# C and D attention of an encoder step: own keys in two column stretches, later keys prepared inside the loop, bias loaded behind the first keys and queries

## The reference, cut to what matters

```python
def attend(q, k, v, bias, mask, sink=None):          # C: windowed, 8 query heads, 2 key heads
    s = jnp.einsum('bqhgd,bkhd->bhgqk', qg, k).astype(F32) * (d ** -0.5)
    s = s.reshape(b, hq, tq, -1) + bias
    s = jnp.where(mask, s, NEG_INF)
    ...                                              # softmax over the keys and the sink, then p @ v
...
def dsa_attend(q, qi, wi, qpos, k, v, ki, kpos, topk, t5_d):   # D: one shared key head
    _, sel = lax.top_k(score, topk)                  # 256 keys per query, chosen by an indexer
    ...                                              # scores of the chosen keys + bias, softmax, times v
```

## Time and profile before

| what | value |
|---|---|
| median of 3 runs | 3963.08 us (3957.71 to 3964.36) |
| the profiled execution: time / span | 3964.57 us / 3962.8 us |
| busy over the span: PE, DVE, ACT, POOL | 92%, 52%, 41%, 18% |
| mean granted TensorE clock | 0.965 |
| C stage, first transfer issued to last output | 2891.1 to 3089.5 us |
| C stage, ahead of the first `scores` | 2891.1 to 2932.1 us |
| D stage, first transfer issued to first `scores` | 3092.6 to 3135.1 us |
| D loop | 3135.1 to about 3705 us |

### The profile page before, as it was taken

The page is one execution under the profiler, slowest core; times in us unless marked ns, Lnnn a source line. Parts: engine busy times, 40 slices in busy tenths (PEclk is TensorE's granted clock), DMA queues, the critical chain, the costliest instruction groups (busy, mean ns, idle before and its releaser), DMA issues. The chain is left out here.

```text
span 3962.8 us, 51485 instructions
## 1 busy us (share of the span) xinstructions
PE 3645.3 (92%) x18001; PEld 2626.6 (66%) x18001; DVE 2065.5 (52%) x5049; ACT 1630.9 (41%) x2532; POOL 693.9 (18%) x474
## 2 busy tenths in 40 slices
PE   5999999996999999998899988899959699999798
PEld 3899989995777666665786654444436465556576
DVE  4211111117887445433331469999958577777522
ACT  5101100013545444443331459998447344444432
POOL 5100000002223111110341100000022332222342
PEclk9999999997999999999999999999979799999899
DMA  6212211214344322321542111101242411100343
GB/s 220 63 68 68 67 66 68 68 57 108 88 109 106 73 68 57 72 51 31 196 162 84 58 39 58 55 33 66 86 113 77 102 36 26 27 24 19 142 164 117
DMA packets 197665, 315.75 MB, mean 80 GB/s; under 512 B 18960, under 2 KB 140200, under 8 KB 191712
## 3 DMA queue, kind: packets, MB, share of 16 engines
q1 hardware_dynamic: 151152, 227.06, 19.5%
q10 hardware_dynamic: 38448, 61.88, 4.3%
q0 software_dynamic: 7824, 23.72, 2.6%
HBM read 207.24 MB, written 105.35 MB: 79 GB/s over the span
## 5 line engine op out<-in xcount | busy, mean ns | idle before, releaser
L1043 PE MATMUL attAB_p_o<-attAB_pt,attAB_v 128*65 128x512 f32 (+4 forms) x1120 | 431.1, 482 | 0.2 <-ACT attAB_pt L1091 0.2
L1131 DVE TENSOR_REDUCE attAB_mx<-attAB_p_s 128x1 f32<-128x512 f32 (+2 forms) x360 | 209.6, 609 | 297.7 <-PE attAB_p_s L976 187.2
L517 DVE COPY ab_stage<-ab_pA 128x256 f32<-128x256 f32 (+2 forms) x108 | 52.7, 488 | 586.6 <-PE ab_pA L486 544.8
L2568 DVE TENSOR_SCALAR_CACHE_REDUCE cd_junk<-score,cd_thr 128x512 bf16<-128x512 f32 (+8 forms) x288 | 350.4, 1275 | 1.4 <-DVE cd_thr L2585 0.3
L2606 ACT ACTIVATE cd_side<-score,cd_thr 128x384 bf16<-128x384 f32 (+2 forms) x192 | 322.3, 1679 | 23.8 <-DVE cd_thr L2585 16.5
L515 ACT ACTIVATE ab_stage<-ab_pA 128x256 f32<-128x256 f32 (+2 forms) x108 | 47.1, 436 | 674.1 <-PE ab_pA L486 655.6
L484 PE MATMUL ab_pA<-ab_W_hi,h_hi 128*128 128x256 f32 x1088 | 309.1, 284 | 3.4 <-PE ab_pA L486 3.2
L1019 PE MATMUL attAB_p_t<-attAB_q_a,attAB_k_a 128*128 128x512 f32 (+4 forms) x560 | 300.3, 540 | 12.7 <-DVE attAB_s_t L1178 11.3
L485 PE MATMUL ab_pA<-ab_W_lo,h_hi 128*128 128x256 f32 x1088 | 307.9, 283 | 0.0
L486 PE MATMUL ab_pA<-ab_W_hi,h_lo 128*128 128x256 f32 x1088 | 307.8, 283 | 0.0
L1672 PE MATMUL attD_p_o<-attD_pt,attD_v 128*65 128x512 f32 (+1 forms) x548 | 282.0, 595 | 1.2 <-ACT attD_pt L1761 1.1
(11 more groups left out here) (353 smaller groups left out, 8538.1 us busy)
## 6 DMA issues: line engine op xcount, KB each, us to landing
ab_W_raw<-in_w_ab SPq DMA_DIRECT2D x17, 1024.0 KB, 5.8
attAB_raw<-t_k SPq DMA_DIRECT2D x32, 544.0 KB, 6.4
attAB_raw<-t_q SPq DMA_DIRECT2D x32, 544.0 KB, 8.4
mix_o<-t_o SPq DMA_DIRECT2D x34, 512.0 KB, 4.3
mix_gate<-t_gate SPq DMA_DIRECT2D x68, 256.0 KB, 4.7
norm_x<-in_x ACTq DMA_DIRECT2D x17, 512.0 KB, 4.3
t_gate<-ab_stage ACTq DMA_DIRECT2D x68, 128.0 KB, 1.7
t_v<-ab_stage ACTq DMA_DIRECT2D x68, 128.0 KB, 1.7
```

The lines of the kernel that those rows point to most:

```text
L1043: done = nc.tensor.matmul(p_o[u % 2][0:VW, i0 * w:(i0 + n) * w], left, pt[c % NPT][:, at * w:(at + n) * w], start=(c == plan.chunks_of[u][ ...
L2568: nc.vector.tensor_scalar(junk[nth % 2][:, 0:widths[n]], sc[n][:], T[:, n:n + 1], None, ALU.is_ge, ALU.add, accum_out=cnt[s % 2][:, n:n + ...
```

## The change

The own keys of 2176 columns are cut at column 768 (six tiles of 128). The key items are ordered: first stretch of every group, second stretch of every group, cached keys of every group. Each item has a semaphore and a place of its own, so no load waits for a split; POOL no longer splits query block 0, DVE does (`split_first_queries`); in C the cached keys have raw tiles of their own, in D the second raw tile.

```diff
+        KEY_CUT = 6 * P
+        own_cols = (slice(0, KEY_CUT), slice(KEY_CUT, ROWS))
+        items = [(g, 0) for g in kvs] + [(g, 1) for g in kvs] + [(g, "cached") for g in kvs]
+        late_at = dict(zip({"C": (4, 6, 10, 12), "D": (3, 24)}[kind], range(NK, 3 * NK)))
+        FIRST_FILLS = 1 if kind == "C" else 2
+
+        def item_needed(u):
+            g, b = group(u % 2), plan.block[u // 2]
+            if b == LAST:
+                return items.index((g, "cached"))
+            return items.index((g, 0 if (b + 1) * P <= KEY_CUT else 1))
...
-                    nc.gpsimd.tensor_tensor(q_a[s][HD:P], q_raw[b % NRAW][HD:P], q_a[s][HD:P].bitcast(F32), ALU.subtract
-                                            ).then_inc(q_split, 1)
+                    if b:
+                        pool.wait_ge(q_split, b)
+                        nc.gpsimd.tensor_tensor(q_a[s][HD:P], q_raw[b % NRAW][HD:P], q_a[s][HD:P].bitcast(F32), ALU.subtract
+                                                ).then_inc(q_split, 1)
...
-                        if u < NK:
-                            pe.wait_ge(key_split, 2 * u + 1)
-                        if plan.block[b] == LAST and x == 0:
-                            pe.wait_ge(key_split, len(items))
+                        pe.wait_ge(key_split, item_needed(u) + 1)
...
+                pe.wait_ge(ident_in, N_IDENT)
-                turn_bias()
...
                     for f in plan.fills_of[u]:
                         fill(f)
+                        if f + 1 == FIRST_FILLS:
+                            turn_bias()
...
                 round_keys(0)
-                for b in plan.early_blocks:
-                    round_queries(b)
-                for m in range(1, len(items)):
+                round_queries(0)
+                for m in range(1, NK):
                     round_keys(m)
...
                 for c in range(NT):
                     exponent(c)
+                    if c in late_at:
+                        round_keys(late_at[c])
...
-                keep_bias()
-                split_keys(0)
-                for m in range(1, len(items)):
-                    split_keys(m)
+                split_keys(0)
+                split_first_queries()
+                for m in range(1, NK):
+                    split_keys(m)
                 for u in plan.early:
                     for f in plan.fills_of[u]:
                         reduce(f)
+                        if f + 1 == FIRST_FILLS:
+                            keep_bias()
                     negate(u)
...
+                    if c in late_at:
+                        split_keys(late_at[c])
```

More of the change, by code:

```diff
@@ L1362, in attention_by_blocks @@
         raw = [sb(f"raw{k}", [P, ROWS]) for k in pair]
+        cached_raw = [sb(f"cached_raw{g}", [P, n_cache * P]) for g in kvs] if kind == "C" else raw[1:2]
         k_a = [sb(f"k_a{g}", [P, ROWS], F32R) for g in kvs]
@@ L1405, in attention_by_blocks @@
             "sink_less", "sink_out", "sinks_set"))
-        raw_in = [sem(f"raw_in{k}") for k in pair]
+        key_in = [sem(f"key_in{m}") for m in range(3 * NK)]
+        ident_in = sem("ident_in")
         q_in = [sem(f"q_in{k}") for k in range(NRAW)]
@@ L1409, in attention_by_blocks, with item_tiles @@
         o_stored = [sem(f"o_stored{k}") for k in pair]
-        N_CONST = 48
+        N_CONST = 32 if kind == "C" else 16
+        N_IDENT = 16 if kind == "C" else 32
         FIXED = 4 * NK + 2 + 2
-        items = [(g, n) for g in kvs for n in range(2)]
+        KEY_CUT = 6 * P
[8 more added lines that the diff above has]
+            return items.index((g, 0 if (b + 1) * P <= KEY_CUT else 1))
+        def item_tiles(m):
+            g, n = items[m]
+            if n == "cached":
+                return cached_raw[g], slice(0, n_cache * P), (c_a[g], c_b[g])
+            return raw[g], own_cols[n], (k_a[g], k_b[g])
         chunks_of_block = lambda b: range(plan.chunks_of[2 * b][0], plan.chunks_of[2 * b + 1][-1] + 1)
@@ L1418, in key_loads @@
             g, n = items[m]
-            if m >= 2:
-                sp.wait_ge(key_split, m - 1)
-            own, cached = key_srcs(g)[0:2]
+            tile, cols, _ = item_tiles(m)
+            src = key_srcs(g)[1] if n == "cached" else key_srcs(g)[0][:, cols]
             for half in (slice(0, HD), slice(HD, P)):
-                if n == 1:
-                    sp.dma_start(raw[m % 2][half, 0:n_cache * P], cached).then_inc(raw_in[m % 2], 16)
-                else:
-                    sp.dma_start(raw[m % 2][half, :], own).then_inc(raw_in[m % 2], 16)
+                sp.dma_start(tile[half, cols], src).then_inc(key_in[m], 16)
         def query_loads(sp, b):
@@ L1476, in _ @@
                     sp.dma_start(sink[:], d.sinks.broadcast_to([P, HEADS])).then_inc(consts, 16)
-                else:
-                    sp.dma_start(identb[:], d.identb).then_inc(consts, 16)
-                key_loads(sp, 0)
-                query_loads(sp, 0)
+                for m in range(1, NK):
+                    key_loads(sp, m)
+                query_loads(sp, 1)
+                for m in range(NK, 2 * NK):
+                    key_loads(sp, m)
                 if kind == "D":
-                    for b in range(NMASK):
+                    for b in range(1, NMASK):
                         mask_loads(sp, b)
-                query_loads(sp, 1)
-                for m in range(1, len(items)):
-                    key_loads(sp, m)
                 for b in range(2, NRAW - 1):
                     query_loads(sp, b)
+                for m in range(2 * NK, 3 * NK):
+                    key_loads(sp, m)
                 for b in range(2, NB):
@@ L1552, in _ @@
                     prepare(b)
+                if kind == "D":
+                    pool.wait_ge(bias_kept, 4)
                 for b in plan.early_blocks:
@@ L1717, in round_keys @@
                 def round_keys(m):
-                    g, n = items[m]
-                    act.wait_ge(raw_in[m % 2], 32 * (m // 2 + 1))
-                    hi, w = ((k_a, ROWS), (c_a, n_cache * P))[n]
-                    nc.scalar.activation(hi[g][:], raw[m % 2][:, 0:w], ACT.Copy).then_inc(key_rounded, 1)
+                    tile, cols, (hi, _) = item_tiles(m)
+                    act.wait_ge(key_in[m], 32)
+                    nc.scalar.activation(hi[:, cols], tile[:, cols], ACT.Copy).then_inc(key_rounded, 1)
                 def round_queries(b):
@@ L1778, in _ @@
                         keep_mask(b, k)
+                for b in plan.early_blocks[1:]:
+                    round_queries(b)
                 for u in plan.early:
@@ L1901, in _ @@
                 dve.wait_ge(fixed, FIXED)
-                dve.wait_ge(consts, N_CONST)
+                dve.wait_ge(ident_in, N_IDENT)
                 nc.vector.tensor_copy(ident_r[:], ident[:]).then_inc(ident_kept, 1)
+                split_keys(0)
+                split_first_queries()
+                for m in range(1, NK):
+                    split_keys(m)
                 if kind == "C":
+                    dve.wait_ge(consts, N_CONST)
                     for k in pair:
```

19 lines of the change are left out of this document (13 added, 6 removed).

## The result

| | before | after |
|---|---|---|
| median | 3961.40 us (4 runs, 3957.71 to 3964.36) | 3936.13 us (4 runs, 3934.65 to 3938.47) |
| ratio after to before | | 0.9936, 95% interval 0.9923 to 0.9948 |
| the profiled execution: span | 3962.8 us | 3933.7 us |
| mean granted TensorE clock | 0.965 | 0.968 |

The forecast started from 3963.08, the median of three executions before; with the fourth it is 3961.40. From 3963.08, the 25.3 us would have led to 3937.8, just inside the range: that the time falls outside is partly chance, the 6.9 us by which the gain was underestimated are not. One execution of the experiment e10 took 7679 us at a granted clock of 0.48 and is left out of its median.

The account below looks back on a forecast made before the run. PE is saturated in the C and D loops but mostly waits ahead of them, so work removed there is worth its time. Gains 8.9 + 14, less loop costs 3 and 1.5, give 18.4 us: 3963.08 to 3945, range 3937 to 3957.

Parts of the forecast that it names:

- C start, -8.9: Ahead of the C loop: unit 2 filled at 2917.3 instead of 2926.17, 8.9 us earlier; bounds 7.5 and 11.5.
- 11.5 us if it lands at 2911: Upper bound of C's start gain: query block 1 lands once only its bytes and the value loads are through.
- D start, -14: Ahead of the D loop: first `scores` at 3121.1 against 3135.07, 14 us earlier; bounds 11.5 and 17.
- I take 3107: Ahead of the D loop: assumed landing time of the bias, between 3104.3 as lower bound and 3109.
- equal shares: D's bias transfer: queues served in turn, values taking half while both are queued; bias at about 3109, sum 2 us smaller.
- PE's first fills behind the turning hold it about 1 us: Ahead of the D loop, after the bias lands: PE's fills delay the first `scores` by about 1 us.
- C loop, +3: Rounding and splitting late keys inside the C loop makes PE lose 3 us; bounds 0 and 7.1.
- D loop, +1.5: Late key work at steps 3 and 24 of the D loop costs 1.5 us; bounds 0.5 and 7.2.
- A, loops in full: Rival, both loops: PE waits for every rounding and split, 14.3 us, giving 3954.5; chance 13%.
- B, late transfers: Rival: D's bias lands at 3109 and C's query block 3 at 2932, 5 us late, giving 3951.7; chance 14%.
- C, slower by the clock: Rival: four large late splits each stop PE until its clock falls, 13.6 us more, giving 3968; chance 3%.
- D, no effect: Rival: something unseen holds each stage's first `scores`, within 4 us of before, giving 3961; chance 5%.

Follow-up runs that it names:

- e10: Changed kernel with SP issuing the value loads behind query blocks 1 to 3, and all four far fills of D's unit 0 ahead of the bias turning; 3933.2 us, 0.9921.
- e2: C stage as changed, D stage written by the former function; 3952.4 us, ratio 0.9978 to the kernel before.
- e3: D stage as changed, C stage written by the former function; 3949.3 us, ratio 0.9963 to the kernel before.
- e4: Changed kernel's order of loads, but all key items rounded and split ahead of the loops, none inside; 3971.6 us, ratio 1.0023 to the kernel before.
- e7: Changed kernel with the value loads issued by SP behind query blocks 1 to 3, instead of by POOL beside the bias; 3933.2 us, 0.9922.
- e1: The changed kernel run again without edit; 3938.1 us, ratio 0.9943 to the kernel before.
- e11: The changed kernel run once more without edit, on another occasion; 3937.3 us, ratio 0.9930 to the kernel before.
- e6: Changed kernel with each late key item rounded twice on ACT and split twice on DVE; 3965.8 us, ratio 1.0005 to the kernel before.
- e9: Changed kernel with late key items rounded and split twice, D's cached keys at step 20 instead of 24; 3960.2 us, ratio 0.9995.

## Why the prediction was right and wrong

**Right: what bounds.** Work ahead of the loops was worth its time and work inside them nearly nothing. e2 and e3 show the gain of each stage by itself, e4 that the new order of loads brings none of it without the move into the loop.

**C start, -8.9, measured -9.5 (-8.3 to -10.7 in the other executions).** The steps hold: block 1 was forecast at 2913.7, T0 + 22.6, and came at T0 + 20.4 to 22.8. e7 shows that its bound, "11.5 us if it lands at 2911, when its bytes and the value loads alone are through", left out the larger lever: with the value loads out of the way, the start is 16 us shorter than before.

**D start, -14, measured -17.3 (-18.4 to -18.7 in e1, e3 and e11). This step failed by size.** Its mechanism was right, two of its terms were not. First, "I take 3107", the landing of the bias at T0 + 14.4: measured T0 + 12.1, near the lower bound that I worked out and passed over (the bytes alone, 3104.3, T0 + 11.7). I had let the value loads of POOL's queue go ahead of the bias. The DMA rows by queue (packets, MB, share), q1 for SP and q0 for POOL, from T0 to the bias, show how far they did. Of the changed kernel:

```profile
q1 hardware_dynamic: 3008, 2.40, 69.0%
q0 software_dynamic: 50, 0.20, 9.8%
```

and of e6, the one execution of this order where the bias came at T0 + 16.0, with all issues ahead of it within 0.4 us of the same times:

```profile
q1 hardware_dynamic: 3193, 2.50, 56.8%
q0 software_dynamic: 261, 0.91, 27.9%
```

0.20 MB of values against 0.91, while SP's queue moved about the same. The others lie between: 0.21 (e1), 0.20 (e11), 0.34 (e3) and 0.49 MB (e9). So the landing lies on either side of what I took: T0 + 12.0 to 12.5 in five of the six executions in which the turning waits for this load alone (the changed kernel, e1, e3, e9 and e11), 16.0 in one. What makes the difference is open. The Trainium skill, "DMA: Bandwidth & Descriptors", section Queues, rings and completion order, has the engines serve queues with work in turn, packet by packet. By equal shares the prediction had made the landing 2 us later than its value. The executions with 0.20 MB do not show equal shares; e6, with 27.9% of the time against 56.8%, comes nearer to them.

Second, "PE's first fills behind the turning hold it about 1 us": no hold, DVE never waited over 0.16 us behind the first copy (8.46 us where 8.7 and 1 were forecast). Together 2.3 + 1.2 = 3.5 us, against the 3.3 that were missing; it is measured from the first reduce, 0.16 us behind the last bias copy. In e1, e3 and e11, where PE reached full clock earlier, the stretch from the bias to `scores` is another 1.0 to 1.2 us shorter.

**C loop, +3, measured +0.8 (0.1 to 1.3 against e4, with e2).** Oversized by 2.2 us: the second term that was mis-sized. I had added up delays of PE of 0.9, 1.4 and 2.0 us over steps 5 to 9. The rows show 0.56 us at step 5 and 0.66 two steps behind the second split: at step 4 DVE was idle for 1.99 us ahead of its split, waiting for ACT, and still caught up; it has 21.4 us of idle time in the 133.

**D loop, +1.5, measured +0.7 (0.2 to 1.1 against e4, 2.9 in e3).** Of the right size in the changed kernel's executions. The 2.9 of e3 come from what the walk left out: DVE's split at step 3 was stretched by POOL's.

**The sum.** 3.3 us of D's start, 2.2 of C's loop, 0.8 of D's loop and 0.6 of C's start are 6.9, which is what the medians miss (25.3 and 18.4). All four errors have one sign: each time I had taken a value on the dear side. Luck worked against the forecast in one more place: the median before fell by 1.7 us with its fourth execution. The range's lower end, 3937, was 2 us above the bounds that I had worked out myself (3935).

**The rivals.** A, loops in full: refuted, the loops grew by 0.8 and 0.7 us where it has 14.3. B, late transfers: block 3 was in time in the changed kernel, ACT rounds it without a wait. But the late bias that B assumed, T0 + 16.4, is what e6 had (16.0): this half of B is real, and came in one of six executions. C, slower by the clock: the mechanism is real. In e9 half clock followed waits of 1.46 and 3.20 us, the latter close to the 2.91 of the earlier trace rows, and in e6 waits of 6.76 and 7.11 us, which cost 9.6 and 10.5 us in all. Waits of 1.97 and 2.50 us in e6's C loop left the clock at 1.00, and so did the waits of 0.6 us behind the late items in the changed kernel and that of 1.67 us in e3. D, no effect: refuted.

## What to carry to other kernels

Where the stretch ahead of a saturated loop is nearly idle and the loop's helpers have a sixth to a quarter of their time free, move into the loop what its first steps don't need; a piece of under 2.5 us cost PE a wait of at most 0.7 us, and 1.67 us the one time that POOL stretched it. Keep each piece small: doubled, the two large pieces of C cost 4.5 us together, and those of D 8 to 10 us each, where the stall also halved PE's clock. And look at what POOL does at that moment: a split beside its instructions lasted two to three times as long. And list what shares the transfer with the last thing that the start waits for, from every queue: taking the value loads out of C's start was worth another 5 to 7 us.

## What the runs showed of the hardware

**In these traces a VectorE and a GpSimd instruction that both read two SBUF tiles do not run at once: one waits for the other to end, and the profile counts its wait as busy time.** In e6 POOL's split of the queries starts at 3179.74 and ends at 3182.09; the first key split of DVE, started at 3179.91, ends at 3184.22, 2.13 us after that. The near tile, started at 3182.16, ends at 3188.14, 3.9 us after the first split (it takes 4.09 alone); the second split, started at 3184.26, ends at 3190.29, 2.15 us after the near tile. At step 3 of e6 the four instructions alternate in the same way. In the changed kernel POOL pays at step 3 of D (its split takes 3.60 us instead of 2.37) and at step 24:

```profile
3159.95 6.03 POOL L1545 TENSOR_TENSOR attD_near<-attD_bias,attD_msk 128x2048 f32<-128x2048 f32 x1
```

It ends 4.0 us behind the end of DVE's split at 3162.01, and nobody waits for it. The Trainium skill, "SBUF — State Buffer", section SBUF: two separate sides, calls the port pair that the two share "an exclusive lock, not a bandwidth split"; these durations agree with it to 0.2 us. I had not put it into the forecast. In the changed kernel's three executions it cost nothing that shows, because DVE began first; that is luck. In e3 POOL began 0.04 us earlier: its split ends at 3129.36 and DVE's at 3130.83, 1.47 us after, so that DVE's split takes 3.80 us and the D loop is the longest of those with one split. In e6 it made four splits 11.2 us longer.

**The share of a second queue varies between executions.** Same order of loads, and issue times of the bias and the values behind T0 within 0.4 us: 0.20 to 0.49 MB of the other queue's data went ahead of the bias in five executions, 0.91 MB in one. The bias landed at T0 + 12.0 to 12.5 and at 16.0, and D's start took 23.8 to 25.1 us and 28.0.
